# A hybrid decoder step: the state products of three heads placed elsewhere in TensorE's program, and the end's first tile added in halves

## What is computed

```
# retention: the state of a head after the 8 new tokens of a sample sequence
kv     = einsum('bnjhd,hj,bnjhe->nbhde', k, w_state, v)
s_last = chunk_decay * s0 + kv          # s0: 8 sequences x 4 heads x 128 x 128

# channel mixer, for every token
g_sel  = argmax(softmax(xf @ w_rg + b_rg))             # group of experts
p_e    = softmax(e_logits of that group)
top_w, top_i = top_k(p_e, 2)
h      = silu(xf @ w_g[e]) * (xf @ w_u[e])
f      = sum over the two chosen e of gate[e] * (h @ w_d[e])
y      = x + g2 * rmsnorm(f)
```

## Time and profile before

| | |
|---|---|
| median of three runs | 597.64 us (596.01 to 602.55) |
| the profiled execution | 593.35 us |
| its span (first to last instruction) | 591.5 us |
| TensorE busy | 556.8 us (94%), 2454 products |
| VectorE, ScalarE, POOL busy | 214.1, 167.9, 110.2 us |
| mean granted clock of TensorE | 0.975 of 2.4 GHz |
| moved from and to memory | 132.96 MB, 225 GB/s |

### The profile page before, as it was taken

One profiled execution on the slowest core, in us unless ns is written; L12 is line 12 of the kernel. 1 busy time (PEld: TensorE's weight loads), 2 busy tenths in 40 slices (PEclk: granted clock), 3 DMA queues, 4 the chain that ended last, 5 costly groups with the idle time before them and its releaser, 6 DMA issues.

```text
span 591.5 us, 6531 instructions
## 1 busy us (share of the span) xinstructions
PE 556.8 (94%) x2454; PEld 338.3 (57%) x2454; DVE 214.1 (36%) x511; ACT 167.9 (28%) x327; POOL 110.2 (19%) x142
## 2 busy tenths in 40 slices
PE   2899999999999999999999987999999999999974
PEld 2557755544454545564444333677776777777621
DVE  2626176421142232442435634423222212221147
ACT  5512586712132231330323333011111111111132
POOL 4105000148000000011101003312323332232100
PEclk9999999999999999999999996699999999999998
DMA  8999857799500000098300367479999999999474
GB/s 302 387 357 316 306 223 320 247 376 292 212 1 0 1 0 0 17 377 266 107 35 13 112 211 262 134 244 336 350 344 319 355 352 336 333 354 345 91 196 162
DMA packets 69557, 132.96 MB, mean 225 GB/s; under 512 B 4526, under 2 KB 41814, under 8 KB 67474
## 3 DMA queue, kind: packets, MB, share of 16 engines
q1 hardware_dynamic: 54576, 99.36, 48.2%
q0 software_dynamic: 9968, 28.56, 17.6%
q10 hardware_dynamic: 4978, 4.58, 2.3%
HBM read 117.28 MB, written 18.35 MB: 229 GB/s over the span
## 4 chain that ended last, share of the span: by engine, by line
PE 89%; DVE 6%; ACT 2%; issue 1%; DMA 1%; ACTq 0%; DVEq 0%
PE psum L690 83%; PE psum L693 6%; DVE arena L2102 1%; ACT arena L1298 1%; DMA hy<-in_c_sample_dram 1%; DVE x L2106 1%; DVE arena L1687 0%; ACT L1298 0%; DVE arena L2024 0%; DVE arena L1973 0%; DVE arena L1718 0%; DVE arena L2157 0%; DVE uT L1694 0%; DVE arena L1985 0%; DVE arena L2224 0%
## 5 line engine op out<-in xcount | busy, mean ns | idle before, releaser
L690 PE MATMUL psum<-ring,arena 128*128 128x256 f32 (+1 forms) x640 | 173.5, 427 | 1.8 <-DVE arena L2157 1.3
L690 PEld LDWEIGHTS psum<-ring,arena 128*128 128x128 f32 x640 | 120.3, 192 | 39.0 <-issue 26.1
L690 PE MATMUL psum<-ring,uT 128*128 128x512 f32 (+1 forms) x384 | 126.8, 522 | 0.4 <-issue 0.4
L1298 ACT ACTIVATE arena<-psum 128x512 f32<-128x512 f32 (+7 forms) x110 | 51.1, 485 | 243.0 <-PE psum L690 223.0
L690 PEld LDWEIGHTS psum<-ring,uT 128*128 128x128 f32 (+1 forms) x384 | 56.5, 172 | 60.8 <-issue 56.5
L690 PE MATMUL psum<-uT,ring 128*128 128x288 f32 x256 | 63.9, 409 | 1.2 <-ACT uT L1298 1.2
L690 PEld LDWEIGHTS psum<-uT,ring 128*128 128x128 f32 x256 | 48.1, 190 | 17.4 <-issue 4.7
L693 PEld LDWEIGHTS psum<-con,arena 128*128 128x128 f32 (+1 forms) x299 | 37.1, 149 | 24.0 <-issue 14.0
L693 PE MATMUL psum<-con,arena 128*128 128x128 f32 (+1 forms) x299 | 43.9, 286 | 5.4 <-DVE arena L1687 2.7
L1298 ACT ACT_TABLE_LOAD x33 | 42.3, 1283 | 3.8 <-DVE eps L1667 2.8
L690 PE MATMUL psum<-arena 128*128 128x128 f32 (+6 forms) x188 | 39.3, 387 | 3.5 <-DMA arena<-f_dram 1.4
(11 more groups left out here) (204 smaller groups left out, 427.9 us busy)
## 6 DMA issues: line engine op xcount, KB each, us to landing
ring<-in_w_mod_dram SPq DMA_DIRECT2D x24, 1024.0 KB, 13.0
ring<-in_w_exp_gate_dram SPq DMA_DIRECT2D x16, 1024.0 KB, 15.2
ring<-in_w_exp_up_dram SPq DMA_DIRECT2D x16, 1024.0 KB, 14.6
ring<-in_w_exp_down_dram SPq DMA_DIRECT2D x16, 1024.0 KB, 12.1
ring<-in_w_in_dram SPq DMA_DIRECT2D x12, 1024.0 KB, 12.1
ring<-in_w_out_dram SPq DMA_DIRECT2D x4, 1024.0 KB, 7.3
f_dram<-in_consts_dram POOLq DMA_DIRECT2D x1, 3072.0 KB
arena<-in_state_ret_dram POOLq DMA_DIRECT2D x6, 512.0 KB, 5.5
```

Source lines behind the costliest of these rows:

```text
L690: return nc.tensor.matmul(out, lhsT, rhs, start=first, stop=last)
L1298: return nc.scalar.activation(out, src, func, **kw).then_inc(done, 1)
```

## The change

Four edits. On TensorE, `add_state(1)` stands directly behind `state_step(1)`, ahead of the sample rows' transposes (`turn_u2(4)`), where it stood behind the last `route_sum`. `state_step(2)` stands behind the last `route_sum`, where it stood behind the branch, and the `keep_running(2)` at that place is gone. `state_step(3)` stands directly behind the branch, ahead of `slot_tokens(1)`, where it stood ahead of `slot_tokens(2)`; and a `keep_running(2)` follows `slot_tokens(1)` as well as `slot_tokens(2)`. At the end, the first tile's sum is added by VectorE in two halves of 512 columns, each when its half of the products is done; `s_comb` counts one more for that, so all later waits on it are one higher.

```diff
--- before.py
+++ after.py
@@ -1121,11 +1121,11 @@
             add_state(0)
             route_sum(3)
             state_step(1)
+            add_state(1)
             turn_u2(4)
             route_parts(4)
             route_sum(4)
-            add_state(1)
-            keep_running(2)
+            state_step(2)
 
 
             pe.wait_ge(s_rsel, 1)
@@ -1239,12 +1239,14 @@
                                   t in ON_DVE)
                         if t not in ON_DVE:
                             last = mm(summed[t][0:n, o], ident[0:n, 0:n], Y[0:n, t, o], False, True)
+                        if t == 0 and c == 0:
+                            last.then_inc(s_comb, 1)
                     last.then_inc(s_comb, 1)
 
+                state_step(3)
                 for e in range(1, AHEAD):
-                    state_step(e + 1)
                     slot_tokens(e)
-                keep_running(2)
+                    keep_running(2)
                 turn_input(0)
                 for e in range(NE):
                     expert_in(e)
@@ -1263,8 +1265,7 @@
                     add_last(t)
             with pe.Else():
 
-                for h in range(2, NH):
-                    state_step(h)
+                state_step(3)
                 wg = ring[:, 0, :].rearrange("p (k n) -> p k n", n=FE)
                 wu = ring[:, 1, :].rearrange("p (k n) -> p k n", n=FE)
                 wd = ring[:, 2, :].rearrange("p (k n) -> p k n", n=D)
@@ -1646,7 +1647,7 @@
                         act.wait_ge(s_f, i + 1)
                         square_f(i, t, Y[:, t])
                     else:
-                        act.wait_ge(s_comb, i + 1)
+                        act.wait_ge(s_comb, i + 2)
                         square_f(i, t, summed[t])
 
         @block.vector
@@ -2219,12 +2220,18 @@
 
                 def add_rest(i, t):
                     n = rows(t)
-                    dve.wait_ge(s_comb, i + 1)
+                    dve.wait_ge(s_comb, i + 2)
                     dve.wait_ge(s_fl[t], 16)
                     v.tensor_tensor(out=Y[0:n, t], in0=summed[t][0:n], in1=Y[0:n, t], op=ALU.add)\
                         .then_inc(s_f, 1)
 
-                add_rest(0, 0)
+                dve.wait_ge(s_fl[0], 16)
+                for c in range(2):
+                    dve.wait_ge(s_comb, c + 1)
+                    o = slice(512 * c, 512 * c + 512)
+                    last = v.tensor_tensor(out=Y[:, 0, o], in0=summed[0][:, o], in1=Y[:, 0, o],
+                                           op=ALU.add)
+                last.then_inc(s_f, 1)
                 add_rest(1, 1)
                 for i, t in enumerate(END_ORDER):
                     finish(i, t, Y[:, t] if t in ON_DVE else summed[t])
```

## The result

Over 20 runs of each kernel the changed kernel takes 592.68 us in the median (589.87 to 599.23) and the kernel before 595.96 (593.38 to 603.29). The ratio is 0.9943 with a 95% interval of 0.9915 to 0.9971: 1.7 to 5.1 us less, 3.4 in the middle. (The ratio leaves out executions more than 1.5% slower than the fastest of their kernel; the medians are of all 20.) That is a small gain, under the 1% bound. The profiled execution took 590.79 us, its span 588.7 against 591.5.

What follows compares the result with a forecast made beforehand. TensorE, with 89% of the chain, was taken as the bound. Terms -0.2, +0.1, -2.36, 0, 0 and +0.3 gave -2.2 us, from 597.64 to 595.4 us; range 592.0 to 599.8, forecast proper 593.8 to 596.9 (62%).

Steps and rivals of the forecast that it cites:

- (1): Ahead of the sample rows' transposes: they start 0.1 us later, a longer-held clock gives back 0.3; net -0.2 us.
- (6): Expert 0's products: they start earlier, but the clock's rise may not move with them; taken as +0.3 us.
- (2): Ahead of the counts: third head's products hidden behind VectorE's picks at no cost; counts perhaps at 1.2 GHz, +0.1 us.
- (3): Behind the branch: `slot_tokens(2)` starts at about 371.7 instead of 374.06, then waiting for VectorE's `hits(2)`; -2.36 us.
- (4): Second head's state stores, queued behind the sample rows' store, do not delay its landing: 0, up to 1.7 us if transfers mix.
- (5): End of the kernel: adding the first tile in halves only lengthens VectorE's idle time; 0, bounded by a gain of 0.6 us.
- The first rival: Passage from mixer to experts: the clock never falls, 7.3 us won, time 590.3 us; chance 8%.
- the slower rival: Expert 0's products: the clock comes back later; a rise at 388 gives +2.2 us, time 599.8 us; chance 8%.
- the two waits named: Gathered rows or sample store land later, meeting the state stores; 1 to 1.7 us go back, 596.4 to 597.1; chance 15%.

Runs made afterwards that it cites:

- the kernel with the identity products alone: Kernel before with only the second head's identity products moved, to between its block products and the sample rows' transposes; ratio 0.9988 to before.
- the variant of four heads: Changed kernel with the fourth head's block products also moved ahead of the counts, directly behind the third head's; ratios 0.9930 and 0.9928 to before.
- the one with the third head's products alone: Changed kernel with the second head's identity products left behind the last logits and the first tile added whole; ratios 0.9892 and 0.9956 to before.
- the variant with the last fillers gone: Changed kernel with the fourth head's block products also ahead of the counts and no fillers behind the third token numbers; ratio 0.9907 to before.

## Why the prediction was right, step by step

The mechanism was right, and so was the direction; the time lay in the range, 2.7 us under the point. Of these 2.7, 597.64 - 595.96 = 1.7 are the level: three runs of before stood 1.7 us above the median of twenty. The rest is a change of -3.3 in the medians where -2.2 was forecast, inside the interval of the ratio. The steps of the first profile give -2.33, those of the second -3.30, and 0.6 of the difference between the two is the clock at expert 0. That -2.33 lies so near -2.2 is in part luck: (1) gave 0.24 more than its term and (6) 0.27 more, and the loads at the end, which the sum did not have, took 0.44.

(1) *Identity products in the wait.* The transposes went back by 0.27 us (354.37 - 352.83 = 1.54 behind VectorE's last instruction, 354.57 - 353.30 = 1.27 in before), near the middle of the bound of 0 to 0.4; I had taken 0.1. The clock gave back 0.27 + 0.44 = 0.71, more than the 0.3 taken and than the 0.6 set as its bound: net -0.44 where -0.2 was forecast. It was mis-sized because I hedged on the clock falling all the same, and the bound was set too low: the transposes alone gave back 0.40 (1.11 to 0.71), the router's products behind them the rest. The clock did not fall there in any of the nine profiles in which the wait was filled, with the identity products or with fillers. Of the three with the wait empty it fell there in two; in the third, *pick* was 8.80, so against that one the filled wait wins only 0.1.

(2) *Third head's products in the shade.* Nothing on the path: they end by 359.2 and TensorE then idles 2.60 us. The counts at 1.2 GHz cost 0.07, forecast 0.1.

(3) *Fillers for products behind the branch.* Forecast -2.36, measured -2.43, of which -2.34 lie between the second and the third token numbers (3.94 us before, 1.60 now). `slot_tokens(2)` now waits 0.24 us for VectorE's marks (released by the line of `hits`), just as the step said. The transposes start above the gathered rows' floor, 369.9.

(4) *State stores.* The sample store landed after 7.2 us where it had 7.3, with the two state stores issued during its flight on the same queue. This is the case that the trace of before could not show. By the rule of turns between queues in the Trainium skill (DMA: Bandwidth & Descriptors, Queues, rings and completion order) nothing was to be expected; the trace agrees, as far as one transfer can. It was the other pair of state stores, those of the third and fourth heads, that came onto the path in the second profile; see (6).

(5) *The end.* 0, as forecast: the whole addition and the halves both give an *end* of 23.2 when the loads are in time. But the reason was only half right. I had the second tile's addition wait for TensorE. In the changed kernel's first profile it waited for its load, and *end* grew by 0.44; in another variant by 1.3 in all. The end is held by two things nearly level with each other, TensorE's last products and the loads of the sums, and I had read it as one.

(6) *The clock at expert 0.* Forecast +0.3, measured +0.03 in the first profile and -0.57 in the second. Over the twelve profiles *e1* went from 10.02 to 11.52, by when the clock rose. Where it rose 3.4 to 5.1 us into the products, the price of 0.5 us for each microsecond holds (in the kernel with the identity products alone 4.7 us slow against 3.4, 0.65 expected and 0.63 measured). Below that it fails: the prediction put the slow 3.4 us of before at a loss of 1.7, but without any slow part *e1* was still 10.02 to 10.30 against 10.69, so that 0.4 to 0.7 came back. The step missed ScalarE's wait for the state stores, shown above, which ends last as soon as the products are fast. The first rival's 1.7 us for expert 0 is too large for the same reason. No profile shows the late clock of the slower rival, a rise more than 8 us into the products (its mark of 2.3 us should have been 2.46, the sum without this term; nothing hangs on it). The variants with the identity products moved show *e1* from 10.12 to 11.52, those without from 10.02 to 10.69: 11.05 against 10.42 in the mean, and seven of the eight lie above all four. That may be a cost of the edit of 0.6 us, more than the 0.44 that it wins ahead of the counts, or chance; the eight also differ in other edits, and four profiles on one side are too few to say.

Of the rivals, the clock that never falls did not come (it fell at 357.7, and at 360.8 in the second profile), and neither of the two waits named ate the gain: the gathered rows had 2 us to spare, and the sample store landed in time. A wait that was not named, ScalarE's for the last state stores, took 1.2 us of TensorE's time in the second profile.

Of the signs that the profile was to show, the wait ahead of the sample rows' transposes is gone, and the third head's products end 2.60 us before the counts. Three lie just outside what was said: the third token numbers come 1.60 us behind the second (1.5 was the limit), expert 0's products 3.28 us earlier, or 2.81 counted from the sample rows (2 to 2.8), and from the first addition to the end of the span it is 20.65 us (20.4).

## What to carry to other kernels

A piece of work that nothing waits for belongs where its engine waits for another, and the gain is bounded by what comes late next: here the first 2.4 us behind the branch were free to take, the next 1.8 came with one more head's products, and then the gathered rows and VectorE's gate weights stood in the way. A store whose landing an engine waits for is such a bound as well, though the data are only an output. Filler products belong only into waits; on the path the last pair cost 0.8 of its 1.0 us. And when an edit is worth less than the scatter of the times, cut the profile into steps between fixed instructions and compare those: the steps in which the clock did not change came out within 0.02 us of each other, where the ratios had an interval of 4 us. The steps that hang on the clock or on loads do not: *e1* scattered by 1.5 us and *end* by 1.3.

## What the runs showed of the hardware that I had not expected

A good part of the scatter between the profiles lies in the first 40 us. In eight of the twelve profiles the granted clock fell for some microseconds between 27 and 35 us, and VectorE's last instruction on the sample rows came at 355.2 to 356.8; in the other four it did not, and it came at 352.8 to 353.4. The same group of 32 input products in the kernel before:

```profile
28.09 8.00 PE L690 MATMUL psum<-uT,ring 128*128 128x288 f32 x32 [1.23 <-ACT uT L1298]
```

and in the changed kernel with the whole addition, where the group starts 0.5 us later, with the clock beside it:

```profile
28.57 10.99 PE L690 MATMUL psum<-uT,ring 128*128 128x288 f32 x32 [1.23 <-ACT uT L1299]
...
28.00:34.00 6.00, 5.43 (x12) 3.90 (x13) 3.28 (x16) 4.10 (x6) 0.30 (x1) 0.50 1.06 309
```

8.00 us against 10.99, and 0.50 granted with TensorE busy for 5.43 of the 6 us. Ahead of both groups stand the same waits of 0.89 and 1.23 us. So programs that are the same up to this point lose 3 us here or not, as much as the whole change is worth. The three kernels that were profiled twice do not show both: the changed kernel had no dip either time, the variant of four heads took 9.60 and 9.58 us, the one with the third head's products alone 9.67 and 10.98. Whether one kernel can have the dip in one execution and not in the next, and whether that is why three runs of before stood 1.7 us off the median of twenty, is therefore not shown.

The other surprise is in the passage itself: groups whose matmuls use 64 rows of the array (the block products) ran back to back for 3.7 us at 1.2 GHz in the changed kernel (365.50 to 369.2) without a rise of the clock at their end. The clock did rise during the 128-row identity products of the same length in before and in the first profile with the third head's products alone, but not in its second. And it rose at 363.1, near the end of the block products of two heads, which use all 128 rows between them, in the variant with the last fillers gone (358.94 to 363.33). What decides it was not tested.
